# A streaming encoder layer on one core: both heads of a query tile in one attention step

## The chip, the cores and the metric

The kernel runs on one core of one Trainium2 chip. The metric is the device time in microseconds (us); the lower, the better. The kernel before takes 1703.53 us, the median of 3 runs (1702.71 to 1705.63).

## The reference, cut to what matters

One layer of a hybrid encoder works on 1024 prompt frames and 32 sample frames with D_MODEL = 1024, all in fp32. After a norm, one combined projection gives pooling input u, q, k, v and two gates. The attention has 8 heads of 64 elements. A chunk of 64 queries sees its own chunk and the 8 preceding ones:

```
def band_attend(q, k, v, q_pos, k_pos, k_valid, rel_bias):
    s = jnp.einsum('bqhd,bkhd->bhqk', q, k).astype(jnp.float32) * (HEAD_DIM ** -0.5)
    rel = jnp.clip(q_pos[:, None] - k_pos[None, :], -REL_CLIP, REL_CLIP) + REL_CLIP
    s = s + rel_bias[:, rel].astype(jnp.float32)[None]
    s = jnp.where(k_valid[None, None, None, :], s, NEG_INF)
    p = jax.nn.softmax(s, axis=-1)
    return jnp.einsum('bhqk,bkhd->bqhd', p.astype(v.dtype), v)
```

The 32 sample frames attend to 512 cached keys and to themselves. The pooling branch (trailing means minus the token, a small linear map), the gates, an output projection, a gated MLP with a convolution of width 3, and a gated side input follow. None of these is changed.

## The kernel before, in words

All activations lie with features on the 128 partitions and the 1056 frames along the free axis. Every projection is done as three fp32r products (high and low halves of weights and input), in pieces of 352 frames: a **chunk** is one tile of 128 output features by 352 frames, 24 matmuls, by `chunk_part` (L514 to L525). There are 60 such chunks. Chunks 0 to 20 come first: v, k and q of the first pair of heads and u. Then 39 slots follow, each with one chunk (21 to 59: v, k and q of the other pairs, then the first four gates) and, up to the last ones, attention work. After them come gates, branches, output projection, MLP and the rest, by `product` (L527, its matmuls in `three`, L510); the first product there is the gate G2p, then the pooling map D0 (`pooled`).

Attention goes by **pairs** of heads (4 pairs; the two heads lie on partitions 0 to 63 and 64 to 127) and by query tiles: 8 tiles of 128 prompt frames, which see 1, 2, 3, 4 and then always 5 key blocks of 128, and a ninth tile of 32 sample frames (544 keys). A **unit** n is one head of one tile; there are 72. In the PE loop (L662 to L680) a slot is two units. An even unit begins with the chunk, and each unit issues `scores(n)`, in even ones `turn_output` of a finished tile, `transposes(n-1)` of the exponentials and `values(n-2)`; in three units of a pair `turn_value` transposes the next pair's v. Scores contract over 64 partitions; transposes and values use all 128. A fp32 matmul shows in the profile as two passes, each with its own weight load; a transpose as one.

The work between these is on two other engines. DVE: `read_scores` (L1151: bias added, running maximum), `invert_sum`, `read_transposes` (L1167: the copy from PSUM to SBUF that `values` waits for), `output_lo`, and the reading of the chunk (`chunk_out`, L1049 and L1051). ACT: `exponentials` (L837), `read_output`, `output_hi`. DVE's order per even unit is scores, sum, transposes, `output_lo`; the chunk is read at the head of the odd unit. PSUM banks: chunks of the slots 0 and 1 in turn, value and output transposes 2, scores 3 and 4 (one unit at a time), transposed exponentials 5 and 6 (one unit at a time), output 7.

Three things stand around the slots. DVE runs `average` (L1091) for each of the four u groups before it begins with the slots. After the last chunk PE waits for `group_split` (L686), the split of the pooling weights that DVE does at L1210 after ACT's share. POOL splits each weight tile (L479, L481), SP loads them.

Of the kernel before, what the change touches and what calls it, by code (L numbers as in the profile page):

```python
# [20 lines left out]
ALU = mybir.AluOpType  # L21
# [4 lines left out]
P = 128  # L26
# [76 lines left out]
TILE_UNITS = 2 * (QT + 1)  # L103
OTILES = QT + 1
UNITS = PAIRS * TILE_UNITS
OUTS = PAIRS * OTILES
CHUNKS = CH * S_JOB
FIRST_CHUNKS = 7 * CH
VT_PARTS = 3
VT_SLOTS = (7, 9, 11)  # L110
# [32 lines left out]
def bank_of(d):  # L143

    if d < 2 * CH:
        return d
    if d < FIRST_CHUNKS:
        return (0, 1, 3, 4)[(d - 2 * CH) % 4]
    return d % 2
# [12 lines left out]
def bank_free(d):  # L162

    if d < 2 * CH + 4:
        return (1, 2, 4, 5)[d - 2 * CH]
    if d < FIRST_CHUNKS:
        return d - 3
    if d < FIRST_CHUNKS + 2:
        return (20, 19)[d - FIRST_CHUNKS]
    return d - 1  # L170


def slot_turns():

    vt = {(0, a): a for a in range(VT_PARTS)}
    ot = {}
    n_turns = VT_PARTS
    for n in range(UNITS + 4):
        i = n % TILE_UNITS
        if n % 2 == 0 and n >= 4:  # L180
            ot[n // 2 - 2] = n_turns
            n_turns += 1
        if i in VT_SLOTS and n // TILE_UNITS + 1 < PAIRS:
            vt[n // TILE_UNITS + 1, VT_SLOTS.index(i)] = n_turns
            n_turns += 1
    return ot, vt, n_turns


TURN_OT, TURN_VT, TURNS = slot_turns()


def build(nc, xT, pT, w_stream, w_group, relr, g_cols, bias_cols, pool_cols, dw_cols, ckT, cv, cpoolT, cconvT,
          o_y, o_pool_p, o_pool_s, o_k, o_v, o_conv):
    ctx = ExitStack()
    with ctx:
# [91 lines left out]
        pt_sb = [at(f"pt_sb{k}", [BAND], F32, b + (2 + k) * BAND * 4) for k in range(2)]  # L287
# [86 lines left out]
        pt_done = sem("pt_done")  # L374
        pt_read = sem("pt_read")
# [35 lines left out]
        def _(sp):  # L411
# [6 lines left out]
            def load_pair(j):  # L418
                if j >= 2:
                    sp.wait_ge(s_read, TILE_UNITS * (j - 1))  # L420
                    sp.wait_ge(pv_done, TILE_UNITS * (j - 1))
# [41 lines left out]
            sp.wait_ge(s_read, 3 * TILE_UNITS)  # L463
            sp.wait_ge(pv_done, 3 * TILE_UNITS)
# [40 lines left out]
        def _(pe):  # L505
# [69 lines left out]
            def turn_value(j, a):  # L575

                n = TURN_VT[j, a]
                if n >= 1:
                    pe.wait_ge(turn_read, n)
                for i in range(3):  # L580
                    b = 3 * a + i
                    m = P if b < QT else NEW
                    mm = pe.transpose(ps_turn[0:m, i * P:(i + 1) * P], vT[j % 2][:, b * P:b * P + m], ident[:])
                mm.then_inc(turn_done, 1)
# [7 lines left out]
            for d in range(3 * CH, FIRST_CHUNKS):  # L592
# [4 lines left out]
                if d < 4 * CH:  # L597
                    turn_value(0, d - 3 * CH)

            def scores(n):  # L600

                j, i = n // TILE_UNITS, n % TILE_UNITS
                t, h = i // 2, i % 2
                rows = slice(h * HEAD, (h + 1) * HEAD)
                if i == 0:
                    pe.wait_ge(chunk_read, FIRST_CHUNKS + 3 * CH * j)
                if n >= 1:
                    pe.wait_ge(s_read, n)
                if t < QT:
                    nb = blocks_of(t)  # L610
                    k0 = (t + 1 - nb) * P
                    q = qT[j % 2][rows, t * P:(t + 1) * P]
                    first = min(nb, 4) * P
                    mm = pe.matmul(ps_s[:, 0:first], q, kT[j % 2][rows, k0:k0 + first], start=True, stop=True)  # L614
                    if nb > 4:
                        mm = pe.matmul(ps_s[:, first:nb * P], q, kT[j % 2][rows, k0 + first:k0 + nb * P], start=True, stop=True)  # L616
                else:
                    pe.wait_ge(pair_loaded[j % 2], 48 * (j // 2) + 48)
                    q = qT[j % 2][rows, SEQ:T]
                    pe.matmul(ps_s[0:NEW, 0:PAST], q, ck_sb[j % 2][rows, :], start=True, stop=True)  # L620
                    mm = pe.matmul(ps_s[0:NEW, PAST:PAST + NEW], q, kT[j % 2][rows, SEQ:T], start=True, stop=True)
                mm.then_inc(s_done, 1)

            def transposes(n):
                t = n % TILE_UNITS // 2
                pe.wait_ge(p_done, n + 1)
                if n >= 1:
                    pe.wait_ge(pt_read, n)
                for b in range(blocks_of(t)):
                    mm = pe.transpose(ps_pt[:, b * P:(b + 1) * P], p_sb[n % 2][:, b * P:(b + 1) * P], ident[:])  # L630
                mm.then_inc(pt_done, 1)

            def values(n):

                j, i = n // TILE_UNITS, n % TILE_UNITS
                t, h = i // 2, i % 2
                cols = slice(h * HEAD, (h + 1) * HEAD)
                if i == 0:
                    pe.wait_ge(turn_read, TURN_VT[j, VT_PARTS - 1] + 1)
                pe.wait_ge(pt_read, n + 1)  # L640
                if h == 0 and n > 0:
                    pe.wait_ge(o_read, n // 2)
                pt = pt_sb[n % 2]
                if t < QT:
                    nb = blocks_of(t)
                    for b in range(nb):
                        mm = pe.matmul(ps_o[:, cols], pt[:, b * P:(b + 1) * P], v_tok[j % 2][:, t + 1 - nb + b, cols],  # L647
                                       start=b == 0, stop=b == nb - 1)
                else:
                    for b in range(PAST // P):  # L650
# [835 lines left out]
```

## Time and profile before

| | us |
|---|---|
| median of 3 runs | 1703.53 |
| the profiled execution | 1703.67 |
| its span, first to last instruction | 1701.9 |
| PE busy | 1646.7 |
| DVE busy | 763.9 |
| POOL busy | 559.3 |
| ACT busy | 292.6 |

The span is shorter than the time of its own execution by 1.8 us. The mean granted clock of TensorE is 0.988 of full speed. The slots run from about 95 us to 431 us of the span. A matmul's duration in the profile includes its way through the array, so durations of successive matmuls overlap; the cost of one is read from the distance between starts. Several instructions of a kind in a row are merged in a timeline, with their count behind x.

### The profile page before, as it was taken

How to read it: one execution, taken by the hardware profiler on the slowest of the kernel's cores; microseconds unless marked ns; L12 is line 12 of the kernel's file. 1: busy time of each engine (PE TensorE's matmuls, PEld its weight loads, DVE VectorE, ACT ScalarE, POOL GpSimd, SP SyncE). 2: the span in 40 equal slices, each digit the busy share in tenths (PEclk: the TensorE clock that was granted, in tenths of full speed). 3: DMA queues.
4: the chain of work that ended last, by engine and by line, in shares of the span. 5: the costliest groups of instructions: out<-in, count | busy, mean ns of one | idle time of the engine just before them, and what ended most of it. 6: DMA issues, size and time to landing. Idle time of an engine off the chain costs nothing.

```text
span 1701.9 us, 23458 instructions
## 1 busy us (share of the span) xinstructions
PE 1646.7 (97%) x10124; PEld 1587.8 (93%) x10124; DVE 763.9 (45%) x972; ACT 292.6 (17%) x513; POOL 559.3 (33%) x282
## 2 busy tenths in 40 slices
PE   7999999999899999999999999999999999999993
PEld 7988888888899999999999999999999999999992
DVE  7654344433223124445543344434434444359555
ACT  5012222222310002122201010010100101013111
POOL 2330201111334343343434434334334334334330
PEclk9999999999999999999999999999999999999996
DMA  6300102100011111312111111111111111111102
GB/s 233 127 27 14 66 14 66 51 19 26 25 48 40 50 39 57 145 39 73 38 50 50 38 50 42 46 50 45 43 50 41 47 50 38 50 51 38 39 25 102
DMA packets 27880, 91.13 MB, mean 54 GB/s; under 512 B 4472, under 2 KB 4480, under 8 KB 27656
## 3 DMA queue, kind: packets, MB, share of 16 engines
q1 hardware_dynamic: 24904, 79.86, 15.1%
q10 hardware_dynamic: 2880, 9.84, 1.5%
q8 instruction: 78, 1.28, 0.3%
q14 instruction: 18, 0.15, 0.0%
HBM read 83.00 MB, written 9.83 MB: 55 GB/s over the span
## 4 chain that ended last, share of the span: by engine, by line
PE 93%; DVE 3%; issue 3%; DMA 1%; ACT 1%; SPq 0%; DVEq 0%; ACTq 0%
PE ps L510 70%; PE ps L522 4%; PE ps L524 4%; PE ps L523 4%; PE ps L614 3%; PE ps L647 3%; PE ps L630 2%; DMA x_in<-xT 1%; PE ps L660 1%; DVE acc L1039 1%; DVE x_res L1391 1%; DVE h_lo L979 1%; PE ps L620 0%; PE ps L616 0%; DVE rms L994 0%
## 5 line engine op out<-in xcount | busy, mean ns | idle before, releaser
L479 POOL TENSOR_TENSOR w_hi<-w_raw,zero 128x1024 fp32r<-128x1024 f32 x122 | 231.1, 1894 | 1080.8 <-PE ps L510 738.3
L510 PE MATMUL ps<-h_hi,w_hi 128*128 128x352 f32 x1536 | 333.7, 325 | 11.0 <-DVE wg_lo L1210 5.3
L510 PE MATMUL ps<-h_hi,w_lo 128*128 128x352 f32 x1536 | 331.5, 323 | 0.0
L510 PE MATMUL ps<-h_lo,w_hi 128*128 128x352 f32 x1536 | 331.3, 324 | 0.0
L481 POOL TENSOR_TENSOR w_lo<-w_raw,w_hi 128x1024 fp32r<-128x1024 f32 x122 | 326.4, 2675 | 9.6
L510 PEld LDWEIGHTS ps<-h_hi,w_hi 128*128 128x128 f32 x1536 | 261.9, 189 | 13.8 <-issue 13.8
L510 PEld LDWEIGHTS ps<-h_hi,w_lo 128*128 128x128 f32 x1536 | 264.1, 188 | 0.0
L510 PEld LDWEIGHTS ps<-h_lo,w_hi 128*128 128x128 f32 x1536 | 261.5, 188 | 0.0
L1275 DVE TENSOR_TENSOR x_res<-ps,x_res 128x1056 f32<-128x1056 f32 x96 | 120.6, 1256 | 148.2 <-PE ps L510 148.2
L522 PE MATMUL ps<-h_hi,w_hi 128*128 128x352 f32 x480 | 161.3, 336 | 8.7 <-DVE w_lo L1021 8.7
L524 PE MATMUL ps<-h_hi,w_lo 128*128 128x352 f32 x480 | 156.2, 325 | 0.0
L523 PE MATMUL ps<-h_lo,w_hi 128*128 128x352 f32 x480 | 156.1, 325 | 0.0
L1151 DVE CUSTOM_DVE_ANT_0 s_sb<-ps,bias_sb 128x640 f32<-128x640 f32 (+5 forms) x72 | 47.5, 659 | 174.4 <-issue 173.7
L510 PE MATMUL ps<-mid_hi,w_hi 128*128 128x352 f32 x528 | 114.2, 324 | 0.0
L510 PE MATMUL ps<-mid_hi,w_lo 128*128 128x352 f32 x528 | 113.8, 323 | 0.0
L510 PE MATMUL ps<-mid_lo,w_hi 128*128 128x352 f32 x528 | 113.7, 323 | 0.0
L522 PEld LDWEIGHTS ps<-h_hi,w_hi 128*128 128x128 f32 x480 | 92.0, 192 | 9.5 <-issue 8.7
L523 PEld LDWEIGHTS ps<-h_lo,w_hi 128*128 128x128 f32 x480 | 92.2, 192 | 0.2
L524 PEld LDWEIGHTS ps<-h_hi,w_lo 128*128 128x128 f32 x480 | 91.8, 191 | 0.0
L510 PEld LDWEIGHTS ps<-mid_hi,w_lo 128*128 128x128 f32 x528 | 90.7, 188 | 0.0
L510 PEld LDWEIGHTS ps<-mid_hi,w_hi 128*128 128x128 f32 x528 | 89.9, 189 | 0.0
L510 PEld LDWEIGHTS ps<-mid_lo,w_hi 128*128 128x128 f32 x528 | 89.7, 188 | 0.0
(170 smaller groups left out, 1831.1 us busy)
## 6 DMA issues: line engine op xcount, KB each, us to landing
w_raw<-w_stream SPq DMA_DIRECT2D x124, 512.0 KB, 3.6
x_in<-xT SPq DMA_DIRECT2D x8, 528.0 KB, 8.6
x_res<-xT ACTq DMA_DIRECT2D x8, 528.0 KB, 8.3
o_y<-x_res ACTq DMA_DIRECT2D x8, 528.0 KB, 2.9
bias_lines<-bias_line SPq DMA_DIRECT2D x1, 3072.0 KB
bias_sb<-bias_lines SPq DMA_DIRECT2D x4, 640.0 KB, 6.5
o_v<-vT SPq DMA_DIRECT2D x4, 272.0 KB, 2.1
o_k<-kT SPq DMA_DIRECT2D x4, 272.0 KB, 2.5
```

The lines of the kernel that those rows point to most:

```text
L479: pool.tensor_tensor(w_hi[k][:], w_raw[k][:], zero[:].broadcast_to([P, KT * P]), ALU.add).then_inc(w_hi_done, 1)
L481: pool.tensor_tensor(w_lo[k][:], w_raw[k][:], w_hi[k][:].bitcast(F32), ALU.subtract).then_inc(w_split, 1)
L510: mm = pe.matmul(out[:, c, :], w, x[:, c * CW:(c + 1) * CW], start=first and n == 0, stop=last and n == 2)
L522: pe.matmul(out, w_hi[k][:, col], x_h, start=b == 0, stop=False)
L523: pe.matmul(out, w_hi[k][:, col], x_l, start=False, stop=False)
L524: mm = pe.matmul(out, w_lo[k][:, col], x_h, start=False, stop=b == KT - 1)
L614: mm = pe.matmul(ps_s[:, 0:first], q, kT[j % 2][rows, k0:k0 + first], start=True, stop=True)
L630: mm = pe.transpose(ps_pt[:, b * P:(b + 1) * P], p_sb[n % 2][:, b * P:(b + 1) * P], ident[:])
L647: mm = pe.matmul(ps_o[:, cols], pt[:, b * P:(b + 1) * P], v_tok[j % 2][:, t + 1 - nb + b, cols], start=b == 0, stop=b == nb - 1)
L660: pe.transpose(ps_turn[:, 0:P], o_tok[:], ident[:]).then_inc(turn_done, 1)
L1151: dve.tensor_tensor_reduce(out=s_sb[n % 2][0:m, 0:nk], in0=ps_s[0:m, 0:nk], in1=bias, scale=-1.0, scalar=BIG, op0=ALU.add, op1=ALU.min, ac ...
L1275: dve.tensor_tensor(by_chunk(x_res[:, m, :]), job_set(job), by_chunk(x_res[:, m, :]), ALU.add).then_inc(evacuated, 1)
```

## The change: what it does

A step m is now a whole query tile with both heads (36 of them), and a slot is one step. PE's order in slot m is: chunk, transposes of tile m-1 (both heads), values of tile m-1 (both heads), scores of tile m (both heads), then the transposes of next values and `turn_output(m-2)`. The scores of the two heads are issued next to each other: 512 keys of head 0, 512 of head 1, then the fifth block of head 0 and of head 1. Head 0 contracts over array rows 0 to 63, head 1 over rows 64 to 127, and they write different PSUM banks (2 and 3; 4 and 5). The exponentials of a tile are transposed in groups of up to four blocks, and all transposes (of exponentials, values and outputs) use banks 1 and 6 in turn; each waits until the last but one has been read. Chunks of the slots all go to bank 0, so each waits until the preceding one has been read. DVE's order in slot m is: `output_lo(m-3)`, the sums, the reading of the chunk, the copies of the transposed groups, the reading of the scores. The `average` of the last u group moves behind the reading of the first scores. PE waits for `group_split` only ahead of D0, behind G2p.

```diff
--- before.py
+++ after.py
...
-    return d % 2
+        return (0, 2, 3, 4)[(d - 2 * CH) % 4]
+    return 0
...
-        return (1, 2, 4, 5)[d - 2 * CH]
+        return (1, 3, 4, 5)[d - 2 * CH]
     if d < FIRST_CHUNKS:
         return d - 3
-    if d < FIRST_CHUNKS + 2:
-        return (20, 19)[d - FIRST_CHUNKS]
-    return d - 1
+    return 19 if d == FIRST_CHUNKS else d
+
+
+def groups_of(m):
+
+    n = 2 * blocks_of(m % OTILES)
+    return [range(i, min(n, i + 4)) for i in range(0, n, 4)]
 
 
 def slot_turns():
 
...
+    turns = {("V", 0, a): a for a in range(VT_PARTS)}
+    n = VT_PARTS
+    for m in range(SLOTS):
+        if 1 <= m <= OUTS:
+            for g in range(len(groups_of(m - 1))):
+                turns["P", m - 1, g] = n
+                n += 1
+        if m % OTILES in VT_SLOTS and m // OTILES + 1 < PAIRS:
+            turns["V", m // OTILES + 1, VT_SLOTS.index(m % OTILES)] = n
+            n += 1
+        if 2 <= m < OUTS + 2:
+            turns["O", m - 2] = n
+            n += 1
+    return turns, n

...
-        pt_sb = [at(f"pt_sb{k}", [BAND], F32, b + (2 + k) * BAND * 4) for k in range(2)]
+        pt_sb = at("pt_sb", [2 * BAND], F32, b + 2 * BAND * 4)
...
-        ps_turn = bank(2)
-        ps_s = ps[:, 3 * 512:3 * 512 + BAND]
-        ps_pt = ps[:, 5 * 512:5 * 512 + BAND]
+        ps_s = [ps[:, 2 * 512:2 * 512 + BAND], ps[:, 4 * 512:4 * 512 + BAND]]
+
+        def ps_turn(n):
+            return bank(1 if n % 2 else 6)
...
+            def scores(m):
+
+                j, t = m // OTILES, m % OTILES
+                heads = [slice(h * HEAD, (h + 1) * HEAD) for h in range(2)]
+                if t == 0:
                     pe.wait_ge(chunk_read, FIRST_CHUNKS + 3 * CH * j)
...
+                if m >= 1:
+                    pe.wait_ge(s_read, 2 * m)
                 if t < QT:
                     nb = blocks_of(t)
                     k0 = (t + 1 - nb) * P
...
                     first = min(nb, 4) * P
...
+                    for h, rows in enumerate(heads):
+                        mm = pe.matmul(ps_s[h][:, 0:first], qT[j % 2][rows, t * P:(t + 1) * P],
+                                       kT[j % 2][rows, k0:k0 + first], start=True, stop=True)
+                        if nb <= 4:
+                            mm.then_inc(s_done, 1)
+                    for h, rows in enumerate(heads if nb > 4 else ()):
+                        pe.matmul(ps_s[h][:, first:nb * P], qT[j % 2][rows, t * P:(t + 1) * P],
+                                  kT[j % 2][rows, k0 + first:k0 + nb * P], start=True, stop=True).then_inc(s_done, 1)
                 else:
                     pe.wait_ge(pair_loaded[j % 2], 48 * (j // 2) + 48)
...
+                    for h, rows in enumerate(heads):
+                        pe.matmul(ps_s[h][0:NEW, 0:PAST], qT[j % 2][rows, SEQ:T], ck_sb[j % 2][rows, :], start=True, stop=True)
+                    for h, rows in enumerate(heads):
+                        pe.matmul(ps_s[h][0:NEW, PAST:PAST + NEW], qT[j % 2][rows, SEQ:T], kT[j % 2][rows, SEQ:T],
+                                  start=True, stop=True).then_inc(s_done, 1)
+
+            def transposes(m, g):
+                nb = blocks_of(m % OTILES)
+                n = TURN["P", m, g]
+                blocks = groups_of(m)[g]
+                pe.wait_ge(p_done, 2 * m + 1 + blocks[-1] // nb)
+                pe.wait_ge(turn_read, n - 1)
+                for i, x in enumerate(blocks):
+                    h, b = x // nb, x % nb
+                    mm = pe.transpose(ps_turn(n)[:, i * P:(i + 1) * P], p_sb[h][:, b * P:(b + 1) * P], ident[:])
+                mm.then_inc(turn_done, 1)

...
+            def values(m, h):
+
+                j, t = m // OTILES, m % OTILES
                 cols = slice(h * HEAD, (h + 1) * HEAD)
...
+                nb = blocks_of(t)
+                if t == 0 and h == 0:
+                    pe.wait_ge(turn_read, TURN["V", j, VT_PARTS - 1] + 1)
+                if h == 0 and m > 0:
+                    pe.wait_ge(o_read, m)
+                for b in range(nb):
+                    x = h * nb + b
+                    if b == 0 or x % 4 == 0:
+                        pe.wait_ge(turn_read, TURN["P", m, x // 4] + 1)
+                    pt = pt_sb[:, x * P:(x + 1) * P]
+                    if t < QT:
+                        mm = pe.matmul(ps_o[:, cols], pt, v_tok[j % 2][:, t + 1 - nb + b, cols], start=b == 0, stop=b == nb - 1)
+                    elif b < PAST // P:
+                        mm = pe.matmul(ps_o[0:NEW, cols], pt[:, 0:NEW], cv_sb[j % 2][:, b, cols], start=b == 0, stop=False)
+                    else:
+                        mm = pe.matmul(ps_o[0:NEW, cols], pt[0:NEW, 0:NEW], v_tok[j % 2][0:NEW, QT, cols], start=False, stop=True)
                 mm.then_inc(pv_done, 1)
...
+            for m in range(SLOTS):
+                d = FIRST_CHUNKS + m
+                if d % CH == 0:
+                    tile_ready(d // CH)
+                pe.wait_ge(chunk_read, bank_free(d))
+                chunk_part(d // CH, d, 0, KT).then_inc(chunk_done, 1)
+                if 1 <= m <= OUTS:
+                    for g in range(len(groups_of(m - 1))):
+                        transposes(m - 1, g)
+                    values(m - 1, 0)
+                    values(m - 1, 1)
+                if m < OUTS:
+                    scores(m)
+                j, t = m // OTILES + 1, m % OTILES
+                if t in VT_SLOTS and j < PAIRS:
                     pe.wait_ge(chunk_read, pair_chunks(j) - 2 * CH)
...
+                    turn_value(j, VT_SLOTS.index(t))
+                if 2 <= m < OUTS + 2:
+                    turn_output(m - 2)
+
+            pe.wait_ge(s_read, 2 * OUTS)
             pe.wait_ge(turn_read, TURNS)
+            pe.wait_ge(o_read, OUTS)
             pe.wait_ge(chunk_read, CHUNKS)
-            pe.wait_ge(group_split, 1)
 
             def pooled(g):
 
+                if g == 0:
+                    pe.wait_ge(group_split, 1)
...
+            for m in range(OUTS + 2):
+                if m >= 3:
+                    output_hi(m - 3)
+                if m >= 2:
+                    read_output(m - 2)
+                if m < OUTS:
+                    exponentials(m, 0)
+                    exponentials(m, 1)
+            output_hi(OUTS - 1)
...
-                chain = average(g, i, chain)
...
+                if i + 1 < PAIRS:
+                    chain = average(g, i, chain)
...
+            def read_transposes(m, g):
+                n = TURN["P", m, g]
+                blocks = groups_of(m)[g]
+                dve.wait_ge(turn_done, n + 1)
+                if m >= 1:
+                    dve.wait_ge(pv_done, 2 * m)
+                dve.tensor_copy(pt_sb[:, blocks[0] * P:(blocks[-1] + 1) * P], ps_turn(n)[:, 0:len(blocks) * P]
+                                ).then_inc(turn_read, 1)
...
+            for m in range(SLOTS):
+                if 3 <= m:
+                    output_lo(m - 3)
+                if 1 <= m <= OUTS:
+                    invert_sum(m - 1, 0)
+                    invert_sum(m - 1, 1)
+                slot_chunk(FIRST_CHUNKS + m)
+                if 1 <= m <= OUTS:
+                    for g in range(len(groups_of(m - 1))):
+                        read_transposes(m - 1, g)
+                if m < OUTS:
+                    read_scores(m, 0)
+                    read_scores(m, 1)
+                j, t = m // OTILES + 1, m % OTILES
+                if t in VT_SLOTS and j < PAIRS:
+                    value_out(j, VT_SLOTS.index(t))
+                if m == 0:
+                    chain = average(U_ORDER[PAIRS - 1], PAIRS - 1, chain)
```

## Rows read from the trace of the kernel before

**Rows 1.** The page: busy time and share of each engine; shares of the chain.

```profile
PE 1646.7 (97%) x10124; PEld 1587.8 (93%) x10124; DVE 763.9 (45%) x972; ACT 292.6 (17%) x513; POOL 559.3 (33%) x282
...
PE 93%; DVE 3%; issue 3%; DMA 1%; ACT 1%; SPq 0%; DVEq 0%; ACTq 0%
```

**Rows 2.** Waits of PE: waited for, us in total, times, longest.

```profile
PE ps L510 <- DVE ple L1375: 1.9, 1, 1.9
```

**Rows 3.** Windows: length, busy of PE, PEld, DVE, ACT, POOL, granted clock, DMA.

```profile
104.00:106.00 2.00, 2.00 (x8) 1.86 (x8) 0.66 (x5) 0.49 (x2) 0.00 (x0) 0.50 0.05 18
...
1552.00:1556.00 4.00, 2.60 (x16) 2.60 (x17) 3.68 (x4) 0.29 (x1) 0.00 (x0) 1.00 0.47 135
```

**Rows 4.** Timeline of PE, one full slot of two units: start, duration, what.

```profile
390.80 0.32 PE L524 MATMUL ps<-h_hi,w_lo 128*128 128x352 f32 x1
...
391.57 0.59 PE L614 MATMUL ps<-kT,qT 64*128 64x512 f32 x1
392.00 0.38 PE L616 MATMUL ps<-kT,qT 64*128 64x128 f32 x2
...
392.48 0.71 PE L630 MATMUL ps<-ident,p_sb 128*128 128x128 f32 x5
393.03 1.23 PE L647 MATMUL ps<-v_tok,pt_sb 128*128 128x64 f32 x10
394.19 1.12 PE L614 MATMUL ps<-kT,qT 64*128 64x512 f32 x2
...
395.46 0.77 PE L630 MATMUL ps<-ident,p_sb 128*128 128x128 f32 x5
396.06 1.23 PE L647 MATMUL ps<-v_tok,pt_sb 128*128 128x64 f32 x10
397.10 0.41 PE L522 MATMUL ps<-h_hi,w_hi 128*128 128x352 f32 x1
```

**Rows 5.** Groups of DVE by shape, 100 to 432 us: busy, mean ns.

```profile
L1167 DVE COPY pt_sb<-ps 128x512 f32<-128x512 f32 x8 | 5.4, 671 | 0.0
...
L1049 DVE TENSOR_TENSOR vT<-ps,rms 128x352 f32<-128x352 f32 x9 | 4.6, 515 | 0.0
...
L1167 DVE COPY pt_sb<-ps 128x256 f32<-128x256 f32 x8 | 3.2, 405 | 0.0
```

**Rows 6.** Timeline of DVE and ACT in the slot of rows 4.

```profile
392.43 0.82 DVE L1151 CUSTOM_DVE_ANT_0 s_sb<-ps,bias_sb 128x640 f32<-128x640 f32 x1 [5.32 <-issue]
...
393.29 0.83 ACT L837 ACTIVATE p_sb<-s_sb,nmax 128x640 f32<-128x640 f32 x1 [0.33 <-DVE nmax L1151]
```

**Rows 7.** Timeline, a copy of transposes that PE waits for.

```profile
420.82 0.71 PE L630 MATMUL ps<-ident,p_sb 128*128 128x128 f32 x5
...
421.57 0.82 DVE L1167 COPY pt_sb<-ps 128x640 f32<-128x640 f32 x1 [4.55 <-PE ps L630]
...
422.45 0.63 PE L651 MATMUL ps<-cv_sb,pt_sb 128*32 128x64 f32 x8
```

**Rows 8.** Timeline of PE and DVE around the first slot.

```profile
99.16 0.32 PE L524 MATMUL ps<-h_hi,w_lo 128*128 128x352 f32 x1
...
101.23 1.30 DVE L1111 SCALAR_TENSOR_TENSOR u_row<-win,u_row 128x1008 f32<-128x1008 f32 x2
...
103.42 0.79 PE L614 MATMUL ps<-kT,qT 64*128 64x128 f32 x2 [3.52 <-DVE nmax L1151]
...
112.97 0.41 PE L522 MATMUL ps<-h_hi,w_hi 128*128 128x352 f32 x1
...
116.97 0.91 PE L614 MATMUL ps<-kT,qT 64*128 64x384 f32 x2
```

**Rows 9.** Timeline of PE after the last chunk.

```profile
436.52 1.22 PE L510 MATMUL ps<-h_hi,w_hi 128*128 128x352 f32 x3 [5.26 <-DVE wg_lo L1210]
...
440.88 0.64 PE L510 MATMUL ps<-h_hi,w_lo 128*128 128x352 f32 x3
441.36 0.65 PE L510 MATMUL ps<-h_hi,w_hi 128*128 128x352 f32 x3
```

More of the change, by code:

```diff
@@ L621, in scores @@
[L621 to L631, printed above, removed]
@@ L633, in values @@
-            def values(n):
-                j, i = n // TILE_UNITS, n % TILE_UNITS
-                t, h = i // 2, i % 2
-                cols = slice(h * HEAD, (h + 1) * HEAD)
[L638 to L650, printed above, removed]
-                        pe.matmul(ps_o[0:NEW, cols], pt[:, b * P:b * P + NEW], cv_sb[j % 2][:, b, cols],
-                                  start=b == 0, stop=False)
-                    mm = pe.matmul(ps_o[0:NEW, cols], pt[0:NEW, PAST:PAST + NEW], v_tok[j % 2][0:NEW, QT, cols],
-                                   start=False, stop=True)
-                mm.then_inc(pv_done, 1)
@@ new lines, in turn_output @@
+            def turn_output(m):
+                n = TURN["O", m]
+                pe.wait_ge(o_read, m + 1)
+                pe.wait_ge(turn_read, n - 1)
+                pe.transpose(ps_turn(n)[:, 0:P], o_tok[:], ident[:]).then_inc(turn_done, 1)
+            for m in range(SLOTS):
[13 more added lines that the diff above has]
+                if t in VT_SLOTS and j < PAIRS:
@@ L850, in read_output, with output_hi @@
                 ins.then_inc(o_read, 1)
[L852 to L864 removed]
+            def output_hi(m):
+                j, t = m // OTILES, m % OTILES
+                rows = P if t < QT else NEW
+                n = TURN["O", m]
+                act.wait_ge(turn_done, n + 1)
+                act.activation(at_hi[:, j, t * P:t * P + rows], ps_turn(n)[:, 0:rows], ACT.Copy).then_inc(at_hi_done, 1)
@@ new lines, in output_lo, with slot_chunk @@
+            def output_lo(m):
+                j, t = m // OTILES, m % OTILES
+                rows = P if t < QT else NEW
+                dve.wait_ge(at_hi_done, m + 1)
+                dve.tensor_tensor(at_lo[:, j, t * P:t * P + rows], ps_turn(TURN["O", m])[:, 0:rows],
+                                  at_hi[:, j, t * P:t * P + rows].bitcast(F32), ALU.subtract).then_inc(turn_read, 1)
+            def slot_chunk(d):
+                s = d // CH
+                if s >= S_GATE:
+                    if s == S_GATE and d % CH == 0:
+                        dve.wait_ge(kv_stored, 32 * (PAIRS - 1))
+                    chunk_out(gate_of((s - S_GATE) // 2)[(s - S_GATE) % 2], d)
+                else:
+                    j, kind = (s - PAIRS) // 3, (s - PAIRS) % 3
+                    if kind < 2 and j >= 2 and d % CH == 0:
+                        dve.wait_ge(kv_stored, 32 * (j - 1))
+                    if kind == 0:
+                        chunk_out(vT[j % 2], d)
+                    elif kind == 1:
+                        chunk_out(kT[j % 2], d)
+                    else:
+                        chunk_out(qT[j % 2], d, SCALE)
```

217 lines of the change are left out of this document (58 added, 159 removed).

## The prediction

> **What bounds the kernel now.** I read the page's busy shares first, then the chain of work that ended last: PE is busy for 97% of the span and holds 93% of the chain, DVE, the next, is at 45% [rows 1]. So a microsecond that PE gains or loses in the slots reaches the end, as long as PE is not made to wait later. Next I looked at PE's waits. There are few, and two of them lie exactly where the change is: 3.52 us before the second unit's scores, because DVE is still in the last `average` [rows 8], and 5.26 us after the last chunk, for the split of the pooling weights [rows 9]. Each also costs clock: after the first the granted clock is 0.50, that is 1.2 GHz instead of 2.4 [rows 3]. A wait of 1.9 us [rows 2] leaves the clock at 1.00 [rows 3]. Last I read one full slot start by start [rows 4], because durations overlap there.
>
> **The passes of a slot** [rows 4]. A pass of 512 columns takes 0.43 us (391.57 to 392.00), a pass of 128 columns or a transpose 0.11, a pass of the values 0.11 to 0.12. Switching the array costs something: a unit's scores are 2 x 0.43 + 2 x 0.11 = 1.08 us of columns, but from 394.19 to the transposes at 395.46 pass 1.27. There is about 0.1 more ahead of the scores (ten values take 1.16 before scores, 1.04 before a chunk), and the five transposes behind take 0.60 instead of 0.55. A visit to the 64-row scores thus costs 0.35 us beside its columns.
>
> **Gain 1, fewer visits.** One visit a tile instead of two. Tiles 0 and 1 are counted in the first stretch below; the other 34 give 34 x 0.35 = 11.9 us.
>
> **Gain 2, two heads at once.** The trace before has no two neighbouring matmuls in different row halves, so this is the unknown of the case. If a half works independently of the other but instructions start in order, the four long passes a, a' (head 0), b, b' (head 1) run as a, then a' beside b, then b': one of four is hidden. For a fifth block, head 0's two short passes also run beside b'. That hides 0.11, 0.21, 0.32 and 0.43 us for tiles of 1 to 4 blocks, 0.64 for each of the four with 5 blocks, and 0.49 for the sample tile: 4.1 us a pair, 16.4 in all. The ends are 0 (no overlap) and half of all score columns, some 29 us a kernel (0.22 + 0.43 + 0.64 + 0.86 + 4 x 1.08 + 0.9 us a pair); below 0 lies the case that a change of half costs like a change of array shape, a rival below. I take 16.4, as the halves share neither partitions of input nor a PSUM bank, and nothing but the order of issue is left to hold them.
>
> The Trainium skill (TensorE: Matmul & The Clock Gate, Part 3: Packing small matmuls) says that matmuls in different row groups overlap, starting a few ns apart, while starts and ends stay in order, and gives 3.07 times the speed for four tiles of K=32. No row here shows it. By that rule the four long passes take three, which is the 16.4 us; without it the sum below would be 16.4 less.
>
> **Loss, the copy of the transposes is laid bare.** Before, transposes and the values that need their copy lie a unit apart. Now one tile's values follow its own transposes at once, and the copy is queued on DVE behind the reading of the chunk, which can start only when the chunk ends. What a copy costs a waiting PE is seen once: transposes at 420.82, whose modelled end is 421.53, are copied from 421.57 to 422.39, and PE goes on at 422.45 [rows 7]; counted from the last column that is 0.20 + 0.82 + 0.06. In the new slot, from the last column of the chunk: 0.20 until DVE starts, 0.52 for the chunk, 0.67 for a group of four blocks [rows 5], 0.06 back: 1.45 us. (For the tile with one block, 0.41 instead of 0.67: 1.19.) PE has in that time only the transposes that fit two banks: 8 x 0.11 = 0.87 us; the third group waits for the first to be read. So it stands still for 0.97, 1.01, 0.80, 0.58 us in tiles of 1 to 4 blocks and 0.58 in each of the other five: 6.3 a pair, 25.0 a kernel, 24.1 without tile 0. After that nothing is late: values are ten passes a head, 1.1 us, and each further copy ends sooner. Is DVE free when the chunk ends? After the scores it reads two heads (2 x 0.82 and small parts), ACT's second exponential ends some 2.8 us after the scores [rows 6], then come the high and the low half of an output and two sums: 3.7 us, against 4.1 for `turn_output` and a chunk (3.99, from 112.97 to 116.97 [rows 8]). The cover is thin but there; 0.2 us more is my bound for this wait (+7 us), 0.1 less the other (-4). That PE stands for 0.6 to 1.0 us should not touch the clock, since 1.9 us did not.
>
> The Trainium skill (TensorEngine Tiling (Array Packing), PSUM Bottleneck) warns that tiling speeds up TensorE and not the reading of PSUM. The rows agree in kind: 1.45 us of waiting against 0.64 saved. Had the copies been hidden, the sum would gain 24.1 us more.
>
> **First slots** [rows 8]. Before, chunk 21 ends at 99.32 and chunk 23 starts at 112.97, with the wait and the slow chunk 22 between. New: scores of tile 0 end near 99.95, chunk 22 runs to 103.95 at full clock. DVE reads chunk 21 by 100.05, sets two masks and reads the scores by 101.3, and does the `average` until 104.4. (It took 6.2 us beside POOL; its long instructions are 1.3 us for the subtraction [rows 8] and as much for the sum, some 3 us in all alone; 6.2 would cost 3 us more.) Then sums, chunk and copy: PE goes on at 105.8, values 0.45, scores of tile 1 with their visit 0.95, chunk 23 near 107.2. Gain 5.8.
>
> **After the last chunk** [rows 9]. Before: 5.26 us idle, 5.4 from the last column, then 15 matmuls in 4.36 us at the low clock where 0.16 each makes 2.4: 7.3 lost. New: chunk 59 waits for the reading of 58 (0.20 + 0.52 + 0.06 less one transpose, 0.7), G2p likewise for that of 59 (0.85). Gain 7.3 - 1.55 = 5.75. What is late next is D0, which needs the split that ended 5.3 us after the last chunk and the d halves 1.4 later; G2p covers 72 x 0.16 = 11.6. Without this cover the gain is gone.
>
> **At nothing:** the changed banks of the first chunks and the wait for `root_done` (read long before, by DVE's order), the SP queue (its waits fall in the same slots), POOL (33% [rows 1]), and equal numbers of matmuls, exponentials and DMAs.
>
> **Sum.** 11.9 + 16.4 - 24.1 + 5.8 + 5.75 = 15.75. From the profiled execution, 1703.67, that leaves 1687.9, say 1688; the median before is 0.14 lower, which is no difference.
>
> **The rivals.**
> - **No overlap of the halves.** Then 16.4 falls away: 1704, no change. For it: no row shows an overlap. Against: separate partitions and banks.
> - **A change of half drains the array** like a change of shape, 0.2 us (a half of a visit and a bit). That is one change in tiles of up to 4 blocks, three in the other five: 19 a pair, 76 in all, 15 us, on top of no overlap: 1719. It decides from 0.01 us a change on, as without overlap the sum is nil. For it: each change of shape does so [rows 4]. Against: the shape, 64 by 128, stays. The Trainium skill (TensorEngine Tiling (Array Packing), Key Properties) says that changing the mode drains and changing the tile does not; by that this rival is out.
> - **DVE comes late to the chunk**, because `output_lo(m-2)` stands ahead of it and waits for ACT behind both exponentials. 0.35 us in each of 36 slots is 12.6 us: 1700. For it: only 0.4 to 0.7 us of cover; against: the durations above, and the shorter tiles have more.
> - **The idle stretches lower the clock in the slots.** A chunk at 1.2 GHz costs 2.4 us more; in a third of the slots it makes 29 us: 1717. Rows 2 and 3 speak against it.
>
> **How the numbers follow.** Overlap as computed 0.62 (1688, itself 1681 to 1694); no overlap 0.16; drain 0.08; DVE late 0.10; clock 0.04. The range reaches from the near half of the greater overlap, 1680, up to the case without overlap with 2 us to spare, 1706. A measurement of this kernel tells about 0.2% (3.4 us) from no change. Faster by more: all of the first case, two thirds of the fourth and a small part of the second, 0.73; within: most of the second and the rest of the fourth, 0.15; slower: the others and the second with a longer wait, 0.12.
>
> **What will show it.** In a slot with five blocks the scores of both heads take 1.5 us of columns (2.15 if there is no overlap), and a start of head 1's first pass together with head 0's second is the overlap itself. PE idles ahead of the third group or the values until DVE's copy of the first group, 0.5 to 1.0 us a slot. The waits at 103 and 436 are gone, the granted clock is 1.00 there, and the first product behind the slots starts about 1 us after the last chunk. A slot of five blocks becomes shorter by 0.4 us (0.35 + 0.64 - 0.58). Wrong would be: equal starts but longer passes, a low clock in the slots, or a new wait at D0.

## The result, and the profile after

The kernel after takes 1679.84 us, the median of 4 runs (1678.51 to 1680.5), against 1703.28 us before in the same session. The ratio is 0.9859 [0.9842, 0.9876]. The gain is 23.4 us. The forecast was 15.7 and the range ended at 1680: the direction was right, the size too small.

The page after, its busy times and the shares of the chain [rows 1]:

```profile
PE 1610.1 (96%) x10124; PEld 1570.1 (94%) x10124; DVE 766.1 (46%) x984; ACT 283.1 (17%) x513; POOL 558.4 (33%) x282
...
PE 91%; DVE 5%; issue 3%; DMA 1%; ACT 0%; SPq 0%; DVEq 0%
```

PE still sets the end, but DVE's share of the chain has grown from 3% to 5%. PE is busy for 36.6 us less with as many instructions, while the span is only 23.2 us shorter; the rest stands in new waits. Waits of PE after: what was waited for, us in total, times, longest.

```profile
PE ps L661 <- DVE pt_sb L1186: 11.3, 16, 0.9
...
PE ps L643 <- DVE pt_sb L1186: 9.0, 20, 0.5
```

These are 36 waits for the copies, one in each of 36 slots, 20.3 us. The waits of 3.52 and 5.26 us [rows 8, 9] are gone. The time a slot takes is read from the start of its scores to the start of the next. One with five blocks, PE after [rows 4]:

```profile
372.21 0.32 PE L529 MATMUL ps<-h_hi,w_lo 128*128 128x352 f32 x1
372.37 1.03 PE L643 MATMUL ps<-ident,p_sb 128*128 128x128 f32 x8
373.85 0.41 PE L643 MATMUL ps<-ident,p_sb 128*128 128x128 f32 x2 [0.44 <-DVE pt_sb L1186]
374.09 2.34 PE L661 MATMUL ps<-v_tok,pt_sb 128*128 128x64 f32 x20
376.37 1.13 PE L620 MATMUL ps<-kT,qT 64*128 64x512 f32 x4
377.33 0.39 PE L625 MATMUL ps<-kT,qT 64*128 64x128 f32 x4
377.65 0.33 PE L672 MATMUL ps<-ident,o_tok 128*128 128x128 f32 x1
```

The scores of both heads, with their visit to the other array shape, end 1.28 us after they began (376.37 to 377.65): as long as those of one head before, 1.27 [rows 4]. The grouped lines say the same over all slots. First the kernel before, from 99.4 to 432 us; then the kernel after, from 100 to 413 us (count, busy time of the group, mean ns of one, idle before):

```profile
L614 PE MATMUL ps<-kT,qT 64*128 64x512 f32 x80 | 44.9, 641 | 0.0
...
L616 PE MATMUL ps<-kT,qT 64*128 64x128 f32 x64 | 12.2, 270 | 0.0
```

```profile
L620 PE MATMUL ps<-kT,qT 64*128 64x512 f32 x80 | 22.6, 641 | 0.0
...
L625 PE MATMUL ps<-kT,qT 64*128 64x128 f32 x64 | 6.2, 270 | 0.0
```

A pass is as long as before, yet together they occupy half the time: every pass of one head lies beside one of the other. DVE in the same slot after (the bracket is its idle time and who ended it):

```profile
372.57 0.53 DVE L1065 TENSOR_TENSOR merged<-ps,rms 128x352 f32<-128x352 f32 x1 [0.86 <-PE ps L529]
373.01 1.71 DVE L1186 COPY pt_sb<-ps 128x512 f32<-128x512 f32 x3
```

From the start of the last chunk matmul to its last column are 0.16 us, so the chunk ends at 372.37 and its reading starts 0.20 later, as said; `output_lo` is not late. The first copy ends about 373.70 and PE goes on at 373.85. The transposes need 8 x 0.11 = 0.88 us from 372.37, so PE's columns stand still for 0.60 us (0.58 was said). The profile shows 0.44, since a duration includes the way through the array: about 0.16 us of each such wait is hidden in it, and 20.3 us shown are 20.3 + 36 x 0.16 = 26 us of lost columns.

The next scores start at 385.62, 9.25 us after 376.37; before, the distance was 10.10 (391.04 [rows 4] to 401.14). The two starts, of after and of before:

```profile
385.62 0.70 PE L620 MATMUL ps<-kT,qT 64*128 64x512 f32 x2
```

```profile
401.14 0.69 PE L614 MATMUL ps<-kT,qT 64*128 64x512 f32 x1
```

That is 0.85 less (0.4 was said): a visit, 0.35, and all of half the columns, 1.08, less the stall of 0.60, make 0.83.

### The profile page after: what moved, and what is told of

It reads as the page before. It is cut to its first block, busy times and chain, and to the rows that moved or that the text cites. A ratio compares the mean times of both kernels' runs of the same rounds, so it can differ in the third digit from the quotient of the medians.

```text
span 1678.7 us, 23495 instructions
## 1 busy us (share of the span) xinstructions
PE 1610.1 (96%) x10124; PEld 1570.1 (94%) x10124; DVE 766.1 (46%) x984; ACT 283.1 (17%) x513; POOL 558.4 (33%) x282
## 3 DMA queue, kind: packets, MB, share of 16 engines
q8 instruction: 78, 1.28, 0.3%
## 4 chain that ended last, share of the span: by engine, by line
PE 91%; DVE 5%; issue 3%; DMA 1%; ACT 0%; SPq 0%; DVEq 0%
PE ps L515 71%; PE ps L527 4%; PE ps L529 4%; PE ps L528 4%; PE ps L661 3%; PE ps L620 2%; DVE pt_sb L1186 1%; PE ps L643 1%; DMA x_in<-xT 1%; DVE acc L1055 1%; DVE x_res L1418 1%; DVE h_lo L995 1%; PE ps L672 0%; DVE rms L1087 0%; DVE rms L1010 0%
## 5 line engine op out<-in xcount | busy, mean ns | idle before, releaser
L945 ACT ACTIVATE conv<-a_row,dw 128x1058 f32<-128x1058 f32 x22 | 28.0, 1274 | 357.7 <-DVE a_row L1025 357.7
```

The costliest lines, as they stand in the source:

```text
L945: act.activation(conv[:], a_row[:, 0:CWID], ACT.Identity, bias=dw[:, f + 3 * FT:f + 3 * FT + 1], scale=dw[:, f:f + 1]).then_inc(conv0_done, 1)
```

## The experiments

All times are medians. Experiments 1 to 4 stood beside the kernel before at 1702.43, experiments 5 to 8 at 1703.26, experiments 9 and 10 at 1705.51; medians of different groups are compared through their ratios. The theory at this point: the two halves of the array run wholly side by side (A). The rival: instructions go in order, and the forecast's other terms are too small (B).

**1. The order of the heads** (after, with head 0's instructions all ahead of head 1's).

```diff
-                        if nb <= 4:
-                            mm.then_inc(s_done, 1)
-                    for h, rows in enumerate(heads if nb > 4 else ()):
-                        pe.matmul(ps_s[h][:, first:nb * P], ...).then_inc(s_done, 1)
+                        if nb > 4:
+                            mm = pe.matmul(ps_s[h][:, first:nb * P], ...)
+                        mm.then_inc(s_done, 1)
```

> The changed kernel, but the scores of head 0 (512 keys and the fifth block) are all issued before those of head 1; the passes are the same. Theory A, each row half has a queue of its own: head 1 still starts with head 0, nothing changes, 1680 us. Theory B, matmuls start strictly in order and one whose half is busy holds back all behind it: head 0's fifth block waits 0.86 us for its own long matmul, and head 1 starts only after it; 0.86 us in 16 tiles with five blocks and 4 sample tiles is 17 us more, 1697 us. Theory of the prediction (only one of four long passes hidden) would leave 1680 with other starts.

Measured: 1679.84 us (1678.91 to 1680.7), ratio 0.9865 [0.9849, 0.9882], as after. PE in the same slot of this kernel:

```profile
376.48 1.14 PE L620 MATMUL ps<-kT,qT 64*128 64x512 f32 x4
377.45 0.39 PE L623 MATMUL ps<-kT,qT 64*128 64x128 f32 x4
377.77 0.33 PE L670 MATMUL ps<-ident,o_tok 128*128 128x128 f32 x1
```

The program has L620, L623 for head 0 and then L620, L623 for head 1. The trace has the four long passes (L620) first, then the four short ones: head 1's long ones begin before head 0's fifth block, which stands ahead of them in the program. In 376.45 to 376.50 alone the timeline already has two passes of L620, since 376.48: as two passes of one head start 0.43 us apart [rows 4], these are of both heads, which start within 0.02 us of each other. So the order between the halves is not the program's, and with it falls the assumption behind 16.4. The Trainium skill (TensorE: Matmul & The Clock Gate, Part 3: Packing small matmuls) says that starts and ends stay in order; this trace does not agree for two row halves. That starts of different row groups lie a few ns apart agrees as far as the timeline resolves it, under 0.02 us here.

**2. Both heads in one half** (after; head 1's scores are left out, head 0's are computed in their place).

```diff
-                heads = [slice(h * HEAD, (h + 1) * HEAD) for h in range(2)]
+                heads = [slice(0, HEAD) for h in range(2)]
```

> The changed kernel, but both heads' scores read partitions 0 to 63, so both lie in the same array half (head 1's scores are left out, head 0's computed twice; all shapes and waits stay). This takes away nothing but the overlap. If the halves run fully side by side: half of all score columns, 29 us more, 1709 us. If only one of four long passes is hidden, as the prediction had it: 16 us more, 1696 us. If the gain came from fewer visits and from the two ends alone: 1680 us.

Measured: 1710.05 us (1709.52 to 1713.98), ratio 1.0049 [1.0032, 1.0065]: 30.2 us above experiment 1. PE, the scores of the same step:

```profile
393.80 1.98 PE L620 MATMUL ps<-kT,qT 64*128 64x512 f32 x4
395.62 0.60 PE L625 MATMUL ps<-kT,qT 64*128 64x128 f32 x4
396.16 0.33 PE L672 MATMUL ps<-ident,o_tok 128*128 128x128 f32 x1
```

The scores take 2.36 us (393.80 to 396.16) in place of 1.28, and the waits for the copies are the same 11.3 and 9.0 us. The overlap is thus worth 30.2 us, the upper end that the prediction gave (some 29), and not 16.4. (Between the profiled executions it is 1708.0 - 1678.7 = 29.3 us; each has one stretch at the lower clock, this one inside the slots, see the last section.) Without it the kernel would be slower than before.

**3. The copies ahead of the chunk's reading on DVE** (after).

```diff
-                slot_chunk(FIRST_CHUNKS + m)
                 if 1 <= m <= OUTS:
                     for g in range(len(groups_of(m - 1))):
                         read_transposes(m - 1, g)
+                slot_chunk(FIRST_CHUNKS + m)
```

> The changed kernel, but DVE copies the transposed groups before it reads the slot's chunk. Theory of the prediction, PE waits because the copy is queued behind the reading of the chunk (0.52 us, less 0.08 overlap): the wait of nearly all 36 slots gets 0.4 us shorter, 16 us less, 1664 us. Rival, the chain of four transposes (0.44), 0.20 to DVE, the copy (0.67) and 0.06 back is as long as that by itself: 1.37 us from the end of the chunk either way; only tiles with one block gain 0.3, so 1679 us.

Measured: 1678.6 us (1677.69 to 1679.62), ratio 0.9856 [0.9839, 0.9872]: 1.2 less than experiment 1, about what the medians can tell, and far from 16. DVE of this kernel, same slot:

```profile
371.80 1.71 DVE L1186 COPY pt_sb<-ps 128x512 f32<-128x512 f32 x3 [1.30 <-PE ps L643]
373.43 0.52 DVE L1065 TENSOR_TENSOR merged<-ps,rms 128x352 f32<-128x352 f32 x1
```

The prediction said that the copy is queued behind the reading of the chunk. It is, but that costs nothing: the copy must first wait for its four transposes. PE of this kernel:

```profile
371.17 1.04 PE L643 MATMUL ps<-ident,p_sb 128*128 128x128 f32 x8
372.64 0.41 PE L643 MATMUL ps<-ident,p_sb 128*128 128x128 f32 x2 [0.44 <-DVE pt_sb L1186]
```

From the chunk's last column to PE's going on are 372.64 - 371.17 = 1.47 us here, and 373.85 - 372.37 = 1.48 after. The chain through four transposes (0.44) is as long as the one through the reading of the chunk (0.44 from start to start). An earlier place in DVE's queue does not hide it; experiment 4 tries other work for PE between transposes and values.

**4. Part of the chunk put there** (after; the first two groups of transposes behind the sixth of the chunk's eight blocks, their copies ahead of the chunk's reading).

```diff
-                chunk_part(d // CH, d, 0, KT).then_inc(chunk_done, 1)
+                chunk_part(d // CH, d, 0, 6)
+                for g in range(early):
+                    transposes(m - 1, g)
+                chunk_part(d // CH, d, 6, KT).then_inc(chunk_done, 1)
...
```

> The changed kernel, but the first two groups of transposes are issued behind the sixth of the chunk's eight blocks, and DVE copies them before it reads the chunk: the last two blocks (6 matmuls, 0.97 us) cover the copy. If the stall in each slot is the chain from transposes to copy to values, nearly all of the 20.3 us that PE waits for these copies goes: 1660 us. If ACT's exponentials are not ready 1 us earlier (they end about 2.6 us after the chunk's start, the sixth block 2.9), or the preceding output is not read yet, new waits take its place and less than half is gained: 1670 us or more.

Measured: 1653.79 us (1652.93 to 1655.34), ratio 0.9713 [0.9696, 0.9729]: 26.0 us below experiment 1. More than was expected, because that was reckoned with the 20.3 us as the profile shows them; with 0.16 a wait, 26 is the whole of it. PE and DVE of this kernel:

```profile
357.39 1.03 PE L643 MATMUL ps<-ident,p_sb 128*128 128x128 f32 x8
358.19 0.41 PE L527 MATMUL ps<-h_hi,w_hi 128*128 128x352 f32 x1
...
359.23 0.38 PE L643 MATMUL ps<-ident,p_sb 128*128 128x128 f32 x2
```

```profile
358.03 1.29 DVE L1190 COPY pt_sb<-ps 128x512 f32<-128x512 f32 x2 [0.35 <-PE ps L643]
359.43 0.53 DVE L1069 TENSOR_TENSOR merged<-ps,rms 128x352 f32<-128x352 f32 x1
```

The six matmuls of the last two blocks cover the copy (no bracket at 359.23). From scores to scores:

```profile
353.08 0.70 PE L620 MATMUL ps<-kT,qT 64*128 64x512 f32 x2
...
361.72 0.70 PE L620 MATMUL ps<-kT,qT 64*128 64x512 f32 x2
```

8.64 us: 1.46 below before's 10.10, and 0.35 + 1.08 = 1.43 was to be had. In a slot of five blocks the visit and the overlap leave nothing to explain. Two new waits of PE for POOL's split of the weights appear in this profile, 1.1 us in all; experiment 9 has none.

**5 and 6. The two moved parts alone, on the kernel before**: the wait for `group_split` behind G2p (5), and the last `average` behind the reading of the first tile's second unit (6).

```diff
-            pe.wait_ge(group_split, 1)
...
+                if g == 0:
+                    pe.wait_ge(group_split, 1)
```

> The kernel before with one part of the change: PE waits for the split of the pooling weights only ahead of D0. By the prediction the 5.4 us wait and the slow clock after it (1.9 us) go, and 0.85 us for the reading of the last chunk stays: 6.5 us less, 1697 us. Rival: D0 or the sigmoids behind it wait instead, and under 2 us are gained, 1702 us.

```diff
-                chain = average(g, i, chain)
+                if i + 1 < PAIRS:
+                    chain = average(g, i, chain)
...
+                if n == 1:
+                    chain = average(U_ORDER[PAIRS - 1], PAIRS - 1, chain)
```

> The kernel before with one part of the change: the average of the last u group runs behind the second reading of scores. By the prediction the wait of 3.5 us and the slow chunk behind it (2.4 us) go, and a wait of up to 1 us for the first copy comes instead: 5 to 6 us less, 1697.5 us. Rival: PE only waits later for DVE, under 2 us are gained.

Measured: 1697.37 us (1695.94 to 1698.04) for 5, ratio 0.9964 [0.9952, 0.9977]: 5.9 us, as the term said (5.75; 6.5 was expected). 1699.93 us (1697.39 to 1701.06) for 6, ratio 0.9978 [0.9968, 0.9987]: 3.3 us where 5.8 was said. Its chunk 23 starts at 107.31, 5.66 us earlier than in the profile before, so the term was right against the execution that it was read from. But in experiment 5, which is the kernel before up to its last chunk, chunk 23 starts at 111.78, 1.2 us earlier than before, behind a shorter stretch at the lower clock; against that the move gains 4.5. In the profiled execution some 2.5 us more were given back later. The last section shows both.

**7. Both moved parts put back** (after): `average` again ahead of the slots, `group_split` again ahead of G2p.

```diff
-                if i + 1 < PAIRS:
-                    chain = average(g, i, chain)
+                chain = average(g, i, chain)
...
-                if m == 0:
-                    chain = average(U_ORDER[PAIRS - 1], PAIRS - 1, chain)
...
+            pe.wait_ge(group_split, 1)
...
-                if g == 0:
-                    pe.wait_ge(group_split, 1)
```

> The changed kernel with both moved parts put back: the average before the slots and the wait for the split before G2p. If the parts add up, it is slower by what the two parts gain alone, some 11 to 12 us: 1691.5 us, and the two-head step alone is worth 12 us. Rival: in the new slots DVE has the time for the average anyway, and only the second part costs: 1686 us.

Measured: 1690.04 us (1689.43 to 1691.15), ratio 0.9923 [0.9906, 0.9939]: the two are worth 10.2 us of the 23.4, the step of two heads 13. PE's waits of this kernel have both again:

```profile
PE ps L515 <- DVE wg_lo L1233: 5.3, 1, 5.3
PE ps L527 <- DVE vT L1064: 3.6, 2, 3.2
```

**8. A second visit to the 64-row shape** (after; head 1's scores behind `turn_output`, which also takes their overlap; in slots 0 and 1 nothing of 128 rows lies between, so 34 slots have a second visit).

```diff
-                    scores(m)
+                    scores(m, (0,))
...
+                if m < OUTS:
+                    scores(m, (1,))
```

> The changed kernel, but head 1's scores are issued behind the 128-row transposes of the output instead of next to head 0's: two visits to the 64-row shape a slot from slot 2 on, and no overlap. By the prediction's terms, with the full overlap: 29 us for the overlap (28 without the first two tiles) and 34 x 0.35 = 12 us for the second visit, 1720 us. If a visit costs nothing once the heads are apart: as with both heads in one half, 1708 us.

Measured: 1729.25 us (1723.9 to 1736.19), ratio 1.0168 [1.0142, 1.0193]. By the ratios this is 20 us above experiment 2, which has no overlap either, but the medians do not give the price of a visit: the runs spread more than any other kernel's, with mean granted clocks from 0.991 down to 0.982, and the profiled one is the fastest. Its span is 1722.1 against 1708.0, 14.1 us, and even there it has one stretch at the lower clock more than experiment 2 (two against one, some 1.6 us each). A single slot is free of that. With five blocks it takes 10.72 us from scores to scores (417.24 to 427.96) where experiment 2 takes 10.34 (393.80 to 404.14): 0.38 for a visit, near the 0.35 that was read from the kernel before.

**9. The split with the ends mended** (experiment 4; chunk 59 in bank 2, the wait for its reading moved ahead of D0, chunk 7 in bank 1).

```diff
-        return (0, 2, 3, 4)[(d - 2 * CH) % 4]
-    return 0
+        return (0, 1 if d == 7 else 2, 3, 4)[(d - 2 * CH) % 4]
+    return 2 if d == CHUNKS - 1 else 0
...
-            pe.wait_ge(chunk_read, CHUNKS)
...
+                    pe.wait_ge(chunk_read, CHUNKS)
...
```

> The kernel with transposes inside the chunk (6 blocks before, 2 behind), and besides: chunk 59 goes to bank 2, so it does not wait for the reading of chunk 58; the wait for the reading of the last chunk stands ahead of D0; chunk 7 goes to bank 1, as before the change. The three waits in the trace of the changed kernel are 0.5, 0.7 and 1.0 us from the last column: 2.2 us less than the kernel without this, 1651.5 us. Rival: DVE is the bound there and the waits come back at D0 and in the early chunks, 1653.8 us.

Measured: 1652.85 us (1649.38 to 1654.11), ratio 0.9698 [0.9681, 0.9714]. The intervals of 4 and 9 overlap, so the 2.6 us between their ratios are not shown. What its trace shows is that the three waits it was built against are gone; one wait for a chunk's reading is left, 0.26 us ahead of chunk 22. It has the lowest ratio of the study and beats both before and after.

**10. The split one block later** (experiment 4 with 7 in place of 6).

```diff
-                chunk_part(d // CH, d, 0, 6)
+                chunk_part(d // CH, d, 0, 7)
```

> The transposes stand behind the seventh block of the chunk, so one block (0.48 us) and the second group of transposes (0.44 with four blocks, 0.22 with two, none with one group) cover the copy of the first group. If the wait is the chain of 0.20 to DVE, 0.67 for the copy and 0.06 back, 0.93 us are needed and 0.92 are there in tiles of four and five blocks, 0.70, 0.48 and 0.48 (of 0.67) in those of 3, 2 and 1: 0.9 us a pair, 3.5 us a kernel more than with the split behind the sixth, 1657.5 us. If any copy exposed costs a fixed restart of PE, all 36 slots lose 0.2 more, 1661 us or above. If the split's place is of no account, 1653.8 us.

Measured: 1661.39 us (1660.14 to 1662.48), ratio 0.9743 [0.9727, 0.9759], some 5 us above experiment 4 by the ratios. That lies between the 3.7 of the chain and the 7.2 or more of a fixed restart, and the medians cannot choose. The slots can: one of five blocks takes 8.79 us from scores to scores (368.62 to 377.41), 0.15 more than the 8.64 of experiment 4, where the chain allowed 0.01. From the first scores to the last, the slots take 277.6 us (99.78 to 377.41), against 270.6 in experiment 4 (99.73 to 370.37): 7.0 more. So every slot loses, as the theory of a fixed restart said. DVE and then PE of this kernel:

```profile
374.05 1.29 DVE L1190 COPY pt_sb<-ps 128x512 f32<-128x512 f32 x2 [0.82 <-PE ps L643]
```

```profile
374.89 0.41 PE L643 MATMUL ps<-ident,p_sb 128*128 128x128 f32 x2
```

Half of the pair of copies is over at about 374.74, and PE goes on 0.15 us later, not the 0.06 of the chain in the prediction. No idle time is shown at 374.89, though the last column of the chunk was at 374.77; again the way through the array covers it.

## Why the prediction was right or wrong

The ledger, in us (medians good to about 1):

| term | predicted | measured | by |
|---|---|---|---|
| two heads at once | 16.4 (0 to 29) | 30.2 | 2 against 1 |
| copies laid bare, tile 0 included | -25.0 | -26.0 | 4 against 1 |
| first slots and after the last chunk | 11.55 | 10.2 | 7 against after |
| fewer visits | 11.9 | 9.0, the rest of 23.4 | by difference; 0.38 a visit by 8 |

The column of the prediction adds up to 14.85 here and not to 15.75: its own sum has the copies at 24.1, with tile 0's wait subtracted in the first slots instead.

- **The step that failed is "Gain 2, two heads at once": the halves do work side by side, but its order of starts was wrong, and with it its size, 13.8 us too small.** It let instructions start in order, so that head 0's second pass kept head 1's first waiting; one of four long passes would be hidden. Experiment 1 shows that each half takes its own instructions, and experiment 2 that all of half the score columns is saved. The prediction had that value as its upper end, and let the range reach only half of the way to it.
- **Fewer visits** was right in a slot (0.35 by experiment 4, 0.38 by experiment 8). The 9.0 is only what the other rows leave over, so it holds whatever else went wrong. It is 2.9 us short, and about 1 more, since tile 0's wait is in both kernels of the 10.2 but is subtracted in the 11.55. Of this, 0.5 is "at nothing: the changed banks of the first chunks". PE at chunk 7, which now shares a bank with chunk 2 and waits for its reading:

```profile
41.42 0.43 PE L527 MATMUL ps<-h_hi,w_hi 128*128 128x352 f32 x1 [0.36 <-DVE vT L1065]
```

- Some 1.6 us more are lost to the clock late in the profiled execution (last section), where the prediction saw no cost, and about 1.1 of the first slots' 5.8 were the longer slow stretch of the one execution it was read from. What is left, under 1 us, stays open; so does how much of either is in the medians.
- **The copies laid bare** came out for a reason that was half wrong, so the match of the sum is in part luck. The chain of 0.20 + 0.52 + 0.67 + 0.06 = 1.45 took 1.48, with 0.15 in place of the last term and 0.44 in place of the reading's 0.52. And the blame on the reading of the chunk fell with experiment 3. The sum was right because the chain through the transposes is as long. (Where the prediction sets 1.45 us of waiting against 0.64 saved, that is the chain; PE's wait is 0.60.)
- **First slots.** The values of tile 0 start at 105.80, as worked out, and chunk 23 starts at 106.99 (107.2 was said, 112.97 before). PE after:

```profile
105.80 0.63 PE L661 MATMUL ps<-v_tok,pt_sb 128*128 128x64 f32 x4 [0.82 <-DVE pt_sb L1186]
106.36 0.70 PE L620 MATMUL ps<-kT,qT 64*128 64x256 f32 x4
106.99 0.43 PE L527 MATMUL ps<-h_hi,w_hi 128*128 128x352 f32 x1
```

- **After the last chunk.** The two short waits are there, chunk 59 for the reading of 58 and G2p for that of 59: with the 0.16 that a bracket hides, 0.67 and 0.98 us, where 0.7 and 0.85 were said, and D0 starts at 424.80 without one. PE after:

```profile
408.18 0.43 PE L527 MATMUL ps<-h_hi,w_hi 128*128 128x352 f32 x1 [0.51 <-DVE merged L1065]
...
413.09 0.72 PE L515 MATMUL ps<-h_hi,w_hi 128*128 128x352 f32 x3 [0.82 <-DVE merged L1065]
```

- **The rivals.** "No overlap" and "a change of half drains the array" fall with 376.37 to 377.65. "DVE comes late" falls with its start 0.20 us after the chunk. "The idle stretches lower the clock in the slots" falls with the granted clock of 1.00 in all three windows of the slots after (columns as in [rows 3]; the clock is the third number from the end):

```profile
96.00:110.00 14.00, 12.92 (x82) 11.88 (x81) 6.89 (x28) 3.98 (x13) 4.29 (x2) 1.00 0.15 43
110.00:405.00 295.00, 275.57 (x1945) 244.51 (x1944) 126.67 (x443) 70.92 (x241) 51.05 (x24) 1.00 0.11 37
405.00:415.00 10.00, 8.67 (x54) 8.13 (x53) 1.40 (x4) 2.27 (x5) 2.50 (x2) 1.00 0.01 2
```

  But this last rival is out for this execution only. In the profiles of experiments 2, 7 and 8, which have the same waits of under 1.2 us in their slots, the clock does fall there (0.57 in 199 to 203, 0.57 in 202 to 206, 0.57 in 281 to 285 and 0.50 in 370 to 373). Experiment 2's tile of three blocks takes 10.06 us there, and 8.40 to 8.46 in the other pairs:

```profile
199.00:203.00 4.00, 4.00 (x17) 4.00 (x17) 0.88 (x5) 1.78 (x7) 1.89 (x1) 0.57 0.12 47
```

  Such a stretch costs 1.6 us there, not the 29 us of the rival.

## What to carry to other kernels

Where no row shows whether two things overlap, the range should hold both ends whole; here 13.8 us lay between the chosen value and the upper end, more than half of the whole gain. Here a copy between two dependent stages of PE cost four transposes + 0.2 + copy + 0.15 us, in either order of DVE; it was hidden by independent matmuls put between the stages (26 us), not by an earlier place in DVE's queue. Read what a wait costs from start to start: an idle column leaves out what the duration of the matmul before it covers, here 0.16 us each time.

## What was not expected of the hardware

- Two fp32 score matmuls in the two row halves run wholly side by side, and a later instruction for the one half starts ahead of an earlier one for the other.
- The same wait of 1.86 us for `ple` [rows 2], which left the clock at 1.00 in the profile before [rows 3], is followed by the lower level in the profile after. The products around it are the same in both. PE at the wait, and the window behind it:

```profile
1528.17 0.75 PE L515 MATMUL ps<-p_hi,w_hi 128*128 128x352 f32 x3 [1.86 <-DVE ple L1402]
```

```profile
1529.00:1533.00 4.00, 4.00 (x17) 4.00 (x16) 1.53 (x3) 1.08 (x1) 0.00 (x0) 0.57 0.03 7
```

  0.57 is 1.2 GHz for most of that window. The restart was at 1553.40 before and is at 1528.17 after, 25.2 us ahead; the last copies of `ple` on DVE (1571.14 and 1547.48) are only 23.7 ahead:

```profile
1571.14 1.26 DVE L1375 COPY ple<-ps 128x1056 f32<-128x1056 f32 x1 [0.40 <-PE ps L510]
```

```profile
1547.48 1.26 DVE L1402 COPY ple<-ps 128x1056 f32<-128x1056 f32 x1 [0.40 <-PE ps L515]
```

  Experiment 6 has the same (granted clock 0.50 behind the wait):

```profile
1550.00:1553.00 3.00, 3.00 (x12) 3.00 (x11) 1.05 (x1) 1.08 (x1) 0.00 (x0) 0.50 0.02 5
```

  It loses 1.6 us there (from the restart at 1548.78 to the last copy of `ple` at 1568.07, against before), and 0.9 behind the last chunk, where 20 matmuls and not 15 run at the lower level after the same 5.3 us of waiting. The program alone does not decide it. Experiment 1 has the instructions of the kernel after there, the same wait of 1.86 us (restart at 1528.31) and the same median, and its profiled execution keeps the clock:

```profile
1529.00:1533.00 4.00, 4.00 (x27) 4.00 (x26) 3.07 (x4) 1.09 (x1) 0.00 (x0) 1.00 0.02 5
```

  Likewise experiment 5, the kernel before up to its last chunk, has the same wait of 3.52 us (restart at 103.31, 103.42 before), but is back at full clock sooner. First experiment 5, then before:

```profile
108.00:110.00 2.00, 2.00 (x12) 1.58 (x11) 0.00 (x0) 0.00 (x0) 0.00 (x0) 1.00 0.00 0
```

```profile
108.00:110.00 2.00, 2.00 (x10) 2.00 (x9) 0.00 (x0) 0.00 (x0) 0.00 (x0) 0.62 0.00 0
```

  So a sentence such as the prediction's, that a wait of 1.9 us leaves the clock alone, or what the clock costs behind a wait, holds for the execution that it was read from. Such stretches, 1 to 1.6 us each, are as large as the spread of one kernel's runs (1678.51 to 1680.50 for the kernel after, whose profile is of the slowest). What decides them was not tried.
- After a semaphore from DVE, PE starts 0.15 us after the end of the instruction that it waited for, in the three places read (373.85, 374.89 and, in experiment 3, 372.64), not 0.06.
